# Eight norms of a fused two-model kernel: filler matmuls in three waits, a one-pass spread, an early root, and normed tiles in PSUM

## What is computed

```
def rmsnorm(x, g):
    y = x * rsqrt(mean(x * x, axis=-1) + EPS)
    return y * g

h = h + gated_deltanet(rmsnorm(h, a_norm), ...)          # norm 0
h = h + conv_ffn(rmsnorm(h, f_norm[0]), ...)             # norm 1
kv = rmsnorm(h, kv_norm) @ w_kv                          # norm 2 (also for b_w_q)
h = h + chunk_attention(...)
h = h + conv_ffn(rmsnorm(h, f_norm[1]), ...)             # norm 3
x = rmsnorm(h, final_norm)                               # norm 4
x = x + g1 * s5_mixer(norm(x) * (1 + sc1) + sh1, ...)    # norm 5
x = x + g2 * mlp(norm(x) * (1 + sc2) + sh2)              # norm 6
x = x + g1 * ssd_mixer(norm(x) * (1 + sc1) + sh1, ...)   # norm 7
x = x + g2 * mlp(norm(x) * (1 + sc2) + sh2)              # norm 8
return rmsnorm(x, final_norm_g)                          # norm 9
```

## Time and profile before

| | |
|---|---|
| median of three runs | 2829.54 us |
| the profiled execution | 2834.37 us |
| its span, first to last instruction | 2832.4 us |
| TensorE busy | 2689.1 us, 95% |
| VectorE, ScalarE, GpSimd busy | 1520.2, 1054.1, 1202.9 us |
| mean granted TensorE clock | 0.958 of full speed |

### The profile page before, as it was taken

One profiled execution on the slowest core, in us unless ns is written; L12 is line 12 of the kernel. 1 busy time (PEld: TensorE's weight loads), 2 busy tenths in 40 slices (PEclk: granted clock), 3 DMA queues, 4 the chain that ended last, 5 costly groups with the idle time before them and its releaser, 6 DMA issues.

```text
span 2832.4 us, 36017 instructions
## 1 busy us (share of the span) xinstructions
PE 2689.1 (95%) x13759; PEld 2207.6 (78%) x13759; DVE 1520.2 (54%) x2025; ACT 1054.1 (37%) x1461; POOL 1202.9 (42%) x548
## 2 busy tenths in 40 slices
PE   7998799999989989999978999999999998999998
PEld 6887667888779667888867878888777877788887
DVE  4473357767585656646576555543554654322224
ACT  4543324333333653333332222232245673232222
POOL 3343243444344544444432135454434666444442
PEclk9999889999999999999989999999999998999999
DMA  4323113345423215555348436553223321222322
GB/s 130 105 75 89 45 45 119 112 134 156 123 86 134 75 46 156 186 163 197 122 134 240 125 109 232 187 184 118 93 74 106 116 93 60 90 90 89 104 89 75
DMA packets 365303, 333.12 MB, mean 118 GB/s; under 512 B 40752, under 2 KB 340208, under 8 KB 365040
## 3 DMA queue, kind: packets, MB, share of 16 engines
q1 hardware_dynamic: 331008, 264.03, 30.3%
q10 hardware_dynamic: 34160, 67.22, 6.7%
HBM read 308.56 MB, written 22.64 MB: 117 GB/s over the span
## 4 chain that ended last, share of the span: by engine, by line
PE 76%; DVE 6%; ACT 2%; issue 2%; DMA 1%; POOL 1%; SPq 0%; ACTq 0%; DVEq 0%; POOLq 0%
PE bank L269 20%; PE bank L271 20%; PE bank L270 20%; PE bank L283 3%; PE bank L284 2%; PE bank L288 2%; PE bank L1724 1%; PE bank L1745 1%; PE bank L1733 1%; PE bank L2419 1%; PE bank L2414 1%; PE bank L384 1%; DVE xt L429 1%; DVE sq_x L354 0%; PE bank L912 0%
## 5 line engine op out<-in xcount | busy, mean ns | idle before, releaser
L259 POOL TENSOR_TENSOR w_lo<-w_raw,w_hi 128x1024 fp32r<-128x1024 f32 x384 | 968.2, 2543 | 1319.5 <-ACT w_hi L207 1303.9
L269 PE MATMUL bank<-x_hi,w_hi 128*128 128x512 f32 x1936 | 764.7, 395 | 5.8 <-DVE m_r L2737 1.9
L270 PE MATMUL bank<-x_lo,w_hi 128*128 128x512 f32 x1936 | 757.2, 391 | 0.0
L271 PE MATMUL bank<-x_hi,w_lo 128*128 128x512 f32 x1936 | 756.6, 391 | 0.0
L207 ACT ACTIVATE w_hi<-w_raw 128x2048 fp32r<-128x2048 f32 x206 | 394.2, 1914 | 857.9 <-PE bank L271 770.7
L269 PEld LDWEIGHTS bank<-x_hi,w_hi 128*128 128x128 f32 x1936 | 366.2, 189 | 85.6 <-issue 7.4
L270 PEld LDWEIGHTS bank<-x_lo,w_hi 128*128 128x128 f32 x1936 | 366.0, 189 | 77.2 <-issue 2.2
L271 PEld LDWEIGHTS bank<-x_hi,w_lo 128*128 128x128 f32 x1936 | 365.8, 189 | 76.7
L269 PE MATMUL bank<-m_hi,w_hi 128*128 128x512 f32 x384 | 149.6, 390 | 0.0
L271 PE MATMUL bank<-m_hi,w_lo 128*128 128x512 f32 x384 | 149.4, 389 | 0.0
L270 PE MATMUL bank<-m_lo,w_hi 128*128 128x512 f32 x384 | 149.4, 389 | 0.0
(11 more groups left out here) (479 smaller groups left out, 4488.4 us busy)
## 6 DMA issues: line engine op xcount, KB each, us to landing
w_raw<-in_mlp_w SPq DMA_DIRECT2D x128, 512.0 KB, 4.4
ada_w<-in_ada_w ACTq DMA_DIRECT2D x96, 512.0 KB, 4.9
w_raw<-in_f_w_up SPq DMA_DIRECT2D x88, 512.0 KB, 5.1
w_raw<-in_m_w_in SPq DMA_DIRECT2D x40, 512.0 KB, 4.7
w_raw<-in_a_w_in SPq DMA_DIRECT2D x32, 512.0 KB, 5.0
w_raw<-in_f_w_down SPq DMA_DIRECT2D x32, 512.0 KB, 4.2
w_raw<-in_w_kv SPq DMA_DIRECT2D x16, 512.0 KB, 4.0
w_raw<-in_s_w_glu SPq DMA_DIRECT2D x16, 512.0 KB, 5.3
```

Source lines behind the costliest of these rows:

```text
L259: op = pool.tensor_tensor(w_lo[s][:, part], w_raw[s][:, part], w_hi[s][:, part].bitcast(F32), ALU.subtract)
L269: pe.matmul(dst, hi_l, hi_r, start=start, stop=False)
L270: pe.matmul(dst, hi_l, lo_r, start=False, stop=False)
L271: return pe.matmul(dst, lo_l, hi_r, start=False, stop=stop)
```

## The change

- `norm_pe` gets nine matmuls whose result nobody reads (`keep_busy`: ones against the identity, 128 columns): one between the two groups of sums (into bank 5), two ahead of the wait for the reciprocal (bank 5), six behind the spread (bank 4). This is done in norms 1 to 8.
- The spread uses `pe.transpose` in place of `pe.matmul`, in norms 0 to 8.
- `root_ready` has ScalarE take a root of one column that nobody reads, ahead of norms 1, 2, 3, 4, 7, 8 and 9. Where the table of the root isn't loaded, it is loaded there.
- `turned=NORM_X` puts `xt` into banks 2 and 3, by turns, in norms 1, 2 (first use), 3, 6, 7 and 8.

```diff
+        NORM_X = (bank[2][:, :], bank[3][:, :])
+        def keep_busy(pe, dst, count):
+            for _ in range(count):
+                pe.matmul(dst[:, 0:P], ones[:, :], ident[:, :], start=True, stop=True)
+
         def norm_pe(pe, c, sqs):
-            norm_sums_pe(pe, c, sqs)
+            norm_sums_pe(pe, c, sqs, warm=True)
+            keep_busy(pe, bank[5], 2)
             norm_spread_pe(pe, c)
+            keep_busy(pe, bank[4], 6)
...
             for j in range(TT):
                 pe.matmul(bank[4][:, j:j + 1], sqs[1][:, j * P:j * P + P], ones[:, 0:1], start=(j == 0), stop=False)
+            if warm:
+                keep_busy(pe, bank[5], 1)
             pe.wait_ge(n_sq, KD * c)
...
             pe.wait_ge(n_rcp, c + 1)
             for j in range(TT):
-                mm = pe.matmul(bank[5][:, j * P:j * P + P], ncol[:, 2, j:j + 1].to_broadcast([P, P]), ident[:, :],
-                               start=True, stop=True)
+                mm = pe.transpose(bank[5][:, j * P:j * P + P], ncol[:, 2, j:j + 1].to_broadcast([P, P]), ident[:, :])
             mm.then_inc(n_bc, 1)
+        def root_ready(act):
+            act.activation(ncol[:, 0, 0:1], eps_col[:, 0:1], ACT.Sqrt)
...
+            x2 = turned or (xt[:, 0, :], xt[:, 1, :])
...
-                    act.activation(dst[:, k, :], xt[:, k % 2, :], ACT.Copy).then_inc(n_hi, 1)
+                    act.activation(dst[:, k, :], x2[k % 2], ACT.Copy).then_inc(n_hi, 1)
...
-                    dve.tensor_tensor(d_lo[:, k, :], xt[:, k % 2, :], d_hi[:, k, :].bitcast(F32),
+                    dve.tensor_tensor(d_lo[:, k, :], x2[k % 2], d_hi[:, k, :].bitcast(F32),
                                       ALU.subtract).then_inc(n_lo, 1)
...
-                dve.scalar_tensor_tensor(xt[:, k % 2, :], h[:, k, :], g(k), RSTD, ALU.mult, ALU.mult).then_inc(n_xt, 1)
+                dve.scalar_tensor_tensor(x2[k % 2], h[:, k, :], g(k), RSTD, ALU.mult, ALU.mult).then_inc(n_xt, 1)
...
                 for i in range(4):
                     n = SLOTS[f"f{f}_dn{c}"] + i
+                    if c == 2 and i == 0:
+                        root_ready(act)
                     split_hi(act, n + 2, i % 2, landed(n - i % 2 + 2))
...
             attn_act(act)
+            root_ready(act)
             b_out_act(act)
-            norm_act(act, 3, 0, 4, slot=SLOTS["f1_up0"])
+            norm_act(act, 3, 0, 4, slot=SLOTS["f1_up0"], turned=NORM_X)
```

More of the change, by code:

```diff
@@ L383, in norm_spread_pe, with norm_hi @@
             for j in range(TT):
-                mm = pe.matmul(bank[5][:, j * P:j * P + P], ncol[:, 2, j:j + 1].to_broadcast([P, P]), ident[:, :],
-                               start=True, stop=True)
+                mm = pe.transpose(bank[5][:, j * P:j * P + P], ncol[:, 2, j:j + 1].to_broadcast([P, P]), ident[:, :])
             mm.then_inc(n_bc, 1)
-        def norm_hi(act, lots, slot, shift=None, ks=range(KD), dst=None):
+        def root_ready(act):
+            act.activation(ncol[:, 0, 0:1], eps_col[:, 0:1], ACT.Sqrt)
+        def norm_hi(act, lots, slot, shift=None, ks=range(KD), dst=None, turned=None):
+            x2 = turned or (xt[:, 0, :], xt[:, 1, :])
             dst = x_hi if dst is None else dst
@@ L403, in norm_act @@
             if split:
-                norm_hi(act, lots, slot, shift)
+                norm_hi(act, lots, slot, shift, turned=turned)
         def norm_root(dve, c):
@@ L409, in norm_root, with norm_dve @@
             dve.wait_ge(n_bc, c + 1)
-        def norm_dve(dve, c, lots, g, shift=None, slot=0, root=True, dst=None):
+        def norm_dve(dve, c, lots, g, shift=None, slot=0, root=True, dst=None, turned=None):
+            x2 = turned or (xt[:, 0, :], xt[:, 1, :])
             d_hi, d_lo = (x_hi, x_lo) if dst is None else dst
@@ L2695, in one @@
                         n = c * PASS + base + i
+                        if c == 3 and i == 4:
+                            root_ready(act)
                         split_hi(act, n + 2, i % 2, landed(n - i % 2 + 2))
@@ L2714, in mlp_act @@
                 turns(act, 3, 1, one)
-                one(3)
+                one(3, end=True)
         def mlp_dve(dve, f, c_norm):
@@ L3412, in _ @@
             onorm_act(act)
+            root_ready(act)
             act_slots(act, "a_out", no_read)
-            norm_act(act, 1, 0, 1, slot=SLOTS["f0_up0"])
+            norm_act(act, 1, 0, 1, slot=SLOTS["f0_up0"], turned=NORM_X)
             s_par_act(act)
             ffn_act(act, 0, 2)
-            norm_act(act, 2, 0, 2, slot=SLOTS["b_k"])
+            norm_act(act, 2, 0, 2, slot=SLOTS["b_k"], turned=NORM_X)
             kv_act(act, 3)
             attn_act(act)
+            root_ready(act)
             b_out_act(act)
-            norm_act(act, 3, 0, 4, slot=SLOTS["f1_up0"])
+            norm_act(act, 3, 0, 4, slot=SLOTS["f1_up0"], turned=NORM_X)
             ffn_act(act, 1, 5)
@@ L3427, in _ @@
             glu_act(act)
-            norm_act(act, 6, 1, 6, shift=lambda k: mod[:, 0, 24 + k:25 + k], slot=SLOTS["p0"])
+            norm_act(act, 6, 1, 6, shift=lambda k: mod[:, 0, 24 + k:25 + k], slot=SLOTS["p0"], turned=NORM_X)
             mlp_act(act, 0)
-            norm_act(act, 7, 1, 7, shift=lambda k: mod[:, 1, k:k + 1], slot=SLOTS["m_in"])
+            norm_act(act, 7, 1, 7, shift=lambda k: mod[:, 1, k:k + 1], slot=SLOTS["m_in"], turned=NORM_X)
             m_in_act(act)
@@ L3433, in _ @@
             gnorm_act(act)
+            root_ready(act)
             act_slots(act, "m_out", no_read)
-            norm_act(act, 8, 1, 8, shift=lambda k: mod[:, 1, 24 + k:25 + k], slot=SLOTS["p1"])
+            norm_act(act, 8, 1, 8, shift=lambda k: mod[:, 1, 24 + k:25 + k], slot=SLOTS["p1"], turned=NORM_X)
             mlp_act(act, 1)
@@ L3482, in _ @@
             add_h_slots(dve, SLOTS["a_out"], 1)
-            norm_dve(dve, 1, 1, lambda k: pcol("f_norm", k), slot=SLOTS["f0_up0"])
+            norm_dve(dve, 1, 1, lambda k: pcol("f_norm", k), slot=SLOTS["f0_up0"], turned=NORM_X)
             s_par_dve(dve)
@@ L3487, in _ @@
                 dve.wait_ge(b_sto[q], 48 * 4)
-            norm_dve(dve, 2, 2, lambda k: pcol("kv_norm", k), slot=SLOTS["b_k"])
+            norm_dve(dve, 2, 2, lambda k: pcol("kv_norm", k), slot=SLOTS["b_k"], turned=NORM_X)
             s_tables_dve(dve)
@@ L3493, in _ @@
             b_out_dve(dve, 3)
-            norm_dve(dve, 3, 4, lambda k: pcol("f_norm", 8 + k), slot=SLOTS["f1_up0"])
+            norm_dve(dve, 3, 4, lambda k: pcol("f_norm", 8 + k), slot=SLOTS["f1_up0"], turned=NORM_X)
             ffn_dve(dve, 1, 4)
@@ L3506, in _ @@
             m_out_dve(dve, 8)
-            norm_dve(dve, 8, 8, lambda k: gainc(1, 8 + k), shift=lambda k: mod[:, 1, 24 + k:25 + k], slot=SLOTS["p1"])
+            norm_dve(dve, 8, 8, lambda k: gainc(1, 8 + k), shift=lambda k: mod[:, 1, 24 + k:25 + k], slot=SLOTS["p1"], turned=NORM_X)
             mlp_dve(dve, 1, 9)
```

14 lines of the change are left out of this document (8 added, 6 removed).

## The result

The changed kernel takes 2812.03 us (median of 6 runs, 2807.45 to 2818.10) against 2828.76 us of the kernel before (6 runs, 2827.82 to 2833.63): 16.7 us or 0.6% faster, ratio 0.9942 with a 95% interval of 0.9929 to 0.9955, which is 12.7 to 20.1 us. The forecast was 2814 us. The profiled execution took 2810.29 us, span 2808.4 us, mean granted clock 0.969 against 0.958. The two profiled executions have spans 24.0 us apart, so a sum taken from the two profiles needn't come to the 16.7 us of the medians.

What follows compares the result with a forecast made beforehand. TensorE, busy 95% of the span, was taken to bound the kernel, losing time in waits and low clock at norms. 7.5 + 1.4 + 12.4 - 5.9 = 15.4 us, so 2829.5 - 15.4 = 2814 us, range 2805 to 2822 (8 in 10: 2805 to 2823).

Steps and rivals of the forecast that it cites:

- Spread, 7.5 us: In the norms' spread, transposes of one pass replace two-pass matmuls, four passes fewer per norm: 7.5 us gained.
- Root ahead, 1.4 us: In norms 3 and 4 the table load no longer stands ahead of the root: 0.7 us each, 1.4 us gained.
- Fillers, 5.9 us lost: In TensorE's waits at the norms, fillers delay the spread and first turn behind them: 5.9 us lost.
- The clock gives back 12.4 us: In the seven first turns, of 14.2 us lost to the low clock, 12.4 us come back.
- The 2.3 us at the low level: In the first turns of norms 5 and 8, 2.3 us each would still run at the low clock.
- PSUM tiles, zero: VectorE writes and reads `xt` in PSUM: taken as zero, between 0.5 us gained per norm and 0.1 lost per operation.
- The bound of 0.5 us per norm: Upper bound for what PSUM tiles gain in a norm by cover from GpSimd: 0.5 us.
- the fourth rival: PSUM traffic in banks 2, 3 and 5 lengthens VectorE's operations; at 0.25 us each it costs 24 us, 2838 us; chance 0.06.
- The prediction's estimate from that page: By the skill's longer PSUM fixed part, each k takes 0.065 us more, the six `turned` turns some 2.5 us more.
- Behind the first turn all stays as it was: After the first turn no loss: the second slot's `w_lo` ends 7 us after the last main matmul, wanted some 17 after.
- the third rival: Part of the gain is lost behind the norm, to a busy ScalarE or later wait: 5 to 8 us less, 2821; chance 0.10.
- Signs: Trace signs at norms and first turns; wrong: unchanged clock, new TensorE idle time after, fillers outlasting `x_hi`, or VectorE's pair above 1.5 us.

Runs made afterwards that it cites:

- e1_no_fill: The changed kernel with no filler matmuls, one-pass spread, early root and PSUM tiles kept: 2817.91 us, ratio 0.9972 to the kernel before.
- e4_fill_turned: The changed kernel with each two-pass filler matmul replaced by two one-pass transposes: 2809.32 us, ratio 0.9946 to the kernel before.
- e2_fill_only: The kernel before with only the nine fillers added at each of norms 1 to 8: 2821.87 us, ratio 0.9981.
- e7_first_two: The changed kernel without the six fillers behind the spread, those of the first two waits kept: 2815.71 us, ratio 0.9958 to the kernel before.
- the move behind norm 1: VectorE's `scol` operations put behind the first slot's two evictions; in the changed kernel, with `ada_acc` operations likewise behind norm 6: 2810.60 us.
- the retuned fillers: Changed kernel, fillers: first wait three (norms 2, 6 six; norm 5 none), seven before norm 2's sums, 22 behind norm 4's spread: 2810.49 us; `ada_acc` behind norm 6's evictions: 2801.15.

## Why the prediction was right, and which steps were off

The time was right to 2 us, and that is in part luck. The mechanism, fillers that carry the clock into the first turn, is the one that the runs show. But the norms and turns gained 19.3 us where the sum had 15.4, and behind the first turns the traces show some 3.5 us lost where it had nothing: two errors of about one size, in opposite directions.

- **Spread, 7.5 us.** Right. From the start of the spread to the first normed tile each norm saves 0.5 to 1.4 us, 8.2 in all eight; put back, it shows 5.1 us in the norms and 8.6 in the run. The forecast's 7.5 lies between these.
- **Root ahead, 1.4 us.** Right: 0.72 us in each of norms 3 and 4, and nothing to see for the early load in norms 2 and 4. This is the whole of it:

```profile
L399 ACT ACT_TABLE_LOAD  x3: 1283/1283/1283, 783.0 to 1419.0; - x3
```

- **Fillers, 5.9 us lost.** Too high. The whole loss is 8.2 + 1.4 - 6.9 = 2.7 us, with 6.9 = 5.8 + 1.1 for what the heads and 4 to 5 gained; e1_no_fill, whose heads are 3.2 us shorter, says nearly the same. I priced six fillers ahead of a cold turn at 0.9 us; they cost 0.4 in norms 2, 5, 6 and 7 and nothing in 1, 3 and 8, where the clock was high or rose while they ran. 0.8 us of the heads' gain is chance: in norm 6 the second sums take 1.05 us where they took 1.86 before. That is no work of the filler ahead of them, since the kernel without fillers has 1.05 too, and the one with transposes as fillers 1.86 (after, e1_no_fill, e4_fill_turned):

```profile
1664.26 1.05 PE L387 MATMUL bank<-ones,sq 128*128 128x1 f32 x8 [1.71 <-DVE sq L355]
...
1668.73 1.05 PE L387 MATMUL bank<-ones,sq 128*128 128x1 f32 x8 [2.03 <-DVE sq L355]
...
1659.13 1.86 PE L387 MATMUL bank<-ones,sq 128*128 128x1 f32 x8 [1.76 <-DVE sq L355]
```

- **The clock gives back 12.4 us.** The turns did shrink by 90.3 - 77.9 = 12.4 us. By the prediction's own rule, length x (1 - clock), they now lose 11.04 x 0.01 + 11.56 x 0.05 = 0.7 us in place of 14.2, so the clock gave back 13.5; the other 1.1 went into turns that are a little longer at the same clock (77.9 - 0.7 = 77.2 against 90.3 - 14.2 = 76.1). That all of the 12.4 arrived needs the tiles in PSUM: with the clock carried as well but the tiles in SBUF the turns shrink by 8.8 (the rest of the change kept) or 11.1 (fillers alone). The 2.3 us at the low level that were to be left in norms 5 and 8 are some 0.2 and 0. And of the four norms in which the clock was to hold with two chances in three, it held in 3 and 8; in 1 and 7 it fell ahead of the spread (spread to first tile 1.10 and 1.16 us, against 0.69) and rose again ahead of the turn.
- **PSUM tiles, zero.** Mis-sized: 3.6 us in the turns by the traces (1.3 beside e2_fill_only, where the tiles come later and the first `x_lo` of norm 1 takes 1.51 us), 6.5 by the medians, some 7 by the ratios 0.9967 and 0.9942, whose intervals just miss each other. The bound of 0.5 us per norm was near it (3 us); I read it as what one operation loses to GpSimd, and left out that a turn at full clock has no slack: 1.3 us each in norms 1 and 3, where 0.5 was the bound. VectorE's write to PSUM costs 8 ns (756 against 748 below), so the fourth rival has no ground. The Trainium skill ("VectorE: DVE Perf Modes", The TRN2 errata) would have had each k longer; the rows above have 684 ns from PSUM and 686 from SBUF. The prediction's estimate from that page should have been 48 k x 0.065 = 3.1 us and not 2.5.

```profile
L444 DVE SCALAR_TENSOR_TENSOR bank<-h,gain,bank x24: 748/756/757, 1666.6 to 2453.4; 128x512 f32<-128x512 f32 x24
...
L444 DVE SCALAR_TENSOR_TENSOR xt<-h,gain,bank x8: 742/748/748, 1469.6 to 1479.2; 128x512 f32<-128x512 f32 x8
```

- **"Behind the first turn all stays as it was"** is the step that failed. I had looked at the second slot's weights only. The third slot waits for an eviction, and that wait grew by 1.4 us in norm 1 (1.75 to 3.15) and 0.5 in norm 6 (2.25 to 2.79); after the latter the clock fell for 3.4 us as well, so norm 6 to norm 7 is 2.1 us longer. Behind norm 1 the gap alone is shown. This is the third rival, smaller than its 5 to 8 us, on top of the forecast's mechanism.
- **Signs.** All four that were named for "right" stand: four passes, PEclk from 0.95 to 1.00, a root gap of 0.04, `xt` and `x_lo` never above 0.8. Of those for "wrong", one stands too, idle time behind the first turn, and it was the one to follow.

**What stays open.** How much of the 19.3 us the run lost can't be told from 16.7: the traces show 1.4 us behind norm 1 and 2.1 behind norm 6, and the stretches far from any norm scatter by more. Norm 7 to norm 8, in which nothing was changed between the two norms but one early root, takes 395.5 to 401.8 us in the fourteen traces, before and after (us, PE busy, PEclk):

```profile
2059.13:2460.97 401.84, 384.72 (x2074) 0.97 0.29 91
...
2042.82:2439.73 396.91, 380.92 (x2075) 0.98 0.29 93
```

The clock is most of this scatter. In this stretch it is low for 17.1 to 27.3 us and TensorE idle for 14.9 to 17.6; less the idle time and half of the low time every trace has 370.7 to 372.8 us. The kernel before was profiled with 27.3 us of it, the one after with 17.1, and that is 5.1 of the 24.0 us between the two profiled executions. Whether the change has a part in it isn't shown. In the same way norm 1 to norm 2 runs from 375.0 to 379.9 us, and from 363.9 to 366.5 without idle and low time.

The six fillers are worth 10.3 us in the norms by e7_first_two and 3.7 in the run, and fillers without the rest 12.8 and 6. The gaps ahead of the third slot and the low clock right behind them come to 3.7 of the first 6.6 missing and 6.2 of the other 6.8; with single profiles set against medians this is an estimate. Whether the move behind norm 1 costs something is open too: TensorE is idle there for 0.5 to 2.1 us more with it, but without it the clock fell for 6.8 us behind the gap of 3.2 in both kernels with the retuned fillers, and not at all in the kernel after.

## What to carry to other kernels

Work that nobody reads, put into a short wait of TensorE ahead of a dense stretch, pays where it holds the clock: look at the granted clock of what follows the wait, not at the wait. When such a stretch gets shorter, ask which buffer its successors' successor needs and who frees it. Here two operations of side work standing ahead of an eviction swallowed part of the gain, and putting them behind it took 5.2 us out of the stretch behind norm 6 in the kernel with the retuned fillers (9 us by the medians) and 4.3 in the kernel after, where the run as a whole gained 1.4 with the move behind norm 1 beside it. Compare single profiles with care: here the clock alone moved one untouched stretch by 5 us. And a tile that VectorE reads beside a busy GpSimd belongs in PSUM when there is a bank free.

## What the runs showed of the hardware

Transposes held and raised TensorE's clock here as matmuls did: 11.0 to 11.6 us a turn with either kind of filler, and 12.3 to 13.7 without the six.

VectorE beside GpSimd: operations with all operands in SBUF stretch from 0.69 to as much as 2.1 us (and of 32 columns from 0.19 to 2.41); with one operand in PSUM none of the 48 of `x_lo` took more than 0.751. Of those 48 only six ran beside `w_lo`, but the whole trace of the kernel after says the same: of VectorE's instructions that ran for over 0.1 us beside a `w_lo` (kinds that occur four times or more), 396 have a tile in PSUM and none took 1.3 times the shortest of its kind; of 268 without one 168 did. A write to PSUM cost VectorE 8 ns, and ScalarE reads the tiles faster: 688 against 724 ns.

```profile
L411 ACT ACTIVATE x_hi<-bank,mod x24: 687/688/692, 1667.4 to 2454.2; 128x512 fp32r<-128x512 f32 x24
L411 ACT ACTIVATE x_hi<-xt,mod x8: 706/724/727, 1470.4 to 1480.0; 128x512 fp32r<-128x512 f32 x8
```

22 fillers behind norm 4's spread didn't help norm 5: after the 6.31 us of idle time that still stood behind them its sums ran at the low level. Here the clock held only where the fillers reached up to the stretch itself.
